# Expert weights as raw float32 in four column tiles of TensorE, 96 token slots per expert

## What is computed

```python
def swiglu(h, w_gate, w_up, w_down):
    return (jax.nn.silu(h @ w_gate) * (h @ w_up)) @ w_down

def moe(h, w_router, w_gate, w_up, w_down):      # h: 256 x 1024
    logits = (h @ w_router).astype(jnp.float32)
    top_l, top_i = lax.top_k(logits, TOP_K)       # 2 of 8
    top_w = jax.nn.softmax(top_l, axis=-1)
    gates = ...                                   # 256 x 8, two entries a row
    y = jnp.zeros_like(h)
    for e in range(N_EXPERTS):                    # w_gate[e], w_up[e]: 1024 x 3584; w_down[e]: 3584 x 1024
        y = y + gates[..., e:e + 1] * swiglu(h, w_gate[e], w_up[e], w_down[e])
    return y
```

## Time and profile before

| | us |
|---|---|
| median of 3 runs (1636.46 to 1638.80) | 1636.68 |
| span of the profiled execution | 1634.3 |
| PE busy | 1602.1 (98%) |
| DVE busy | 1253.7 (77%) |
| ACT busy | 1055.6 (65%) |
| mean rate of the DMA | 278 GB/s |
| first expert matmul starts at | 600.53 |
| last expert matmul starts at | 1621.31 |

### The profile page before, as it was taken

The page is one execution under the profiler, slowest core; times in us unless marked ns, Lnnn a source line. Parts: engine busy times, 40 slices in busy tenths (PEclk is TensorE's granted clock), DMA queues, the critical chain, the costliest instruction groups (busy, mean ns, idle before and its releaser), DMA issues.

```text
span 1634.3 us, 28652 instructions
## 1 busy us (share of the span) xinstructions
PE 1602.1 (98%) x9254; PEld 1368.5 (84%) x9254; DVE 1253.7 (77%) x1418; ACT 1055.6 (65%) x1214; POOL 103.2 (6%) x130
## 2 busy tenths in 40 slices
PE   8999999999999989999999999999999999999997
PEld 7999899998999868887887887888888888888885
DVE  6665755456574669889879889888888988987986
ACT  5454444444554447777777767768777777777874
POOL 0640000000451010000000000000000000000000
PEclk9999999999999979999999999999999999999999
DMA  9654455565554919989998998997997998998980
GB/s 323 214 192 145 144 196 188 187 198 165 186 178 130 335 62 330 378 311 340 377 333 329 374 350 310 373 369 284 382 362 286 384 362 283 382 372 308 350 314 26
DMA packets 230156, 453.95 MB, mean 278 GB/s; under 512 B 8384, under 2 KB 74208, under 8 KB 230112
## 3 DMA queue, kind: packets, MB, share of 16 engines
q1 hardware_dynamic: 230112, 453.33, 77.8%
HBM read 452.26 MB, written 1.05 MB: 277 GB/s over the span
## 4 chain that ended last, share of the span: by engine, by line
PE 96%; DVE 1%; ACT 1%; issue 0%; DMA 0%; POOL 0%; SPq 0%; POOLq 0%; DVEq 0%
PE bank L1195 94%; PE bank L1587 1%; DMA gain<-in_ln_dram 0%; PE bank L1312 0%; POOL rs L1131 0%; DVE mem L696 0%; ACT mem L460 0%; DVE mem L977 0%; ACT w_hi L437 0%; ACT xt_hi L466 0%; DVE x L725 0%; PE bank L1610 0%; PE bank L1228 0%; PE bank L1341 0%; PE bank L1289 0%
## 5 line engine op out<-in xcount | busy, mean ns | idle before, releaser
L663 DVE TENSOR_TENSOR w_lo<-mem,w_hi 128x1024 fp32r<-128x1024 f32 x854 | 1007.0, 1228 | 223.9 <-ACT w_hi L437 222.8
L437 ACT CAST w_hi<-mem 128x1024 fp32r (+1 forms) x854 | 863.9, 1050 | 300.4 <-PE bank L1195 293.1
L1195 PE MATMUL bank<-w_hi,xt_hi 128*128 128x512 f32 (+1 forms) x1088 | 421.5, 387 | 0.9 <-DVE xt_lo L1036 0.9
L1195 PE MATMUL bank<-w_hi,xt_lo 128*128 128x512 f32 (+1 forms) x1088 | 417.2, 383 | 0.0
L1195 PE MATMUL bank<-w_lo,xt_hi 128*128 128x512 f32 (+1 forms) x1088 | 417.1, 383 | 0.0
L1195 PE MATMUL bank<-w_hi,area 128*128 128x512 f32 x1072 | 350.5, 397 | 1.5 <-DVE area L1098 1.5
L1195 PE MATMUL bank<-xt_hi,w_hi 128*128 128x256 f32 x880 | 249.8, 284 | 2.9 <-DVE w_lo L663 2.1
L1195 PE MATMUL bank<-xt_lo,w_hi 128*128 128x256 f32 x880 | 249.3, 283 | 0.0
L1195 PE MATMUL bank<-xt_hi,w_lo 128*128 128x256 f32 x880 | 248.5, 282 | 0.0
L1195 PEld LDWEIGHTS bank<-w_hi,area 128*128 128x128 f32 x1072 | 201.9, 188 | 49.9 <-issue 1.7
L1195 PEld LDWEIGHTS bank<-w_hi,xt_lo 128*128 128x128 f32 x1088 | 205.4, 189 | 44.2
(11 more groups left out here) (173 smaller groups left out, 910.1 us busy)
## 6 DMA issues: line engine op xcount, KB each, us to landing
mem<-in_eg_dram SPq DMA_DIRECT2D x112, 1024.0 KB, 6.5
mem<-in_eu_dram SPq DMA_DIRECT2D x112, 1024.0 KB, 6.5
mem<-in_ed_dram SPq DMA_DIRECT2D x112, 1024.0 KB, 6.4
mem<-in_w_in_dram SPq DMA_DIRECT2D x42, 1024.0 KB, 5.5
mem<-in_fg_dram SPq DMA_DIRECT2D x11, 1024.0 KB, 5.2
mem<-in_fu_dram SPq DMA_DIRECT2D x11, 1024.0 KB, 5.2
mem<-in_fd_dram SPq DMA_DIRECT2D x11, 1024.0 KB, 4.8
mem<-in_w_br_dram SPq DMA_DIRECT2D x8, 1024.0 KB, 4.9
```

The costliest lines, as they stand in the source:

```text
L437: nc.scalar.copy(w_hi[:, q % H, :], src).then_inc(hi_done, 1)
L663: nc.vector.tensor_tensor(w_lo[:, q % H, :], src, w_hi[:, q % H, :].bitcast(F32), ALU.subtract).then_inc(lo_done, 1)
L1195: return nc.tensor.matmul(out, lhs, rhs, start=first, stop=last, skip_group_check=True)
```

## The change

The experts no longer split their weights. PE multiplies raw float32 weights from the ring with raw float32 activations, in float32 matmuls of two passes. SLOTS falls from 128 to 96, in GROUPS = 3 groups of 32 tokens. For a group, the same 32 columns of `ex` are loaded into four column tiles of the array (the output's partitions 32q to 32q+31 name the tile), and each tile streams another quarter (256 columns) of the weights' 1024. A **half** is the new name of a piece of 128 x 1024: it takes 3 groups x 4 tiles = 12 matmuls, 24 passes.

The hidden width is cut in four steps (1024, 1024, 1024 and 512 columns) instead of seven. The ring of the expert stage has RM = 21 halves; neighbouring halves are loaded together in one 1 MB transfer where they lie together, rows are 4 KB (2 KB in the last step, and in all gate and up transfers before), and SP waits for PE's `half_used` where it waited for DVE's `lo_done`. The gather is made of float32 matmuls, without high and low parts; the output is still split in two, and the scatter uses four row tiles of 32 slots. ACT and DVE keep silu, product, copies and the residual. The casts of L589 and L1186 go, and so do the splits of the first pieces; DVE's routing has a few more small operations, since with 96 slots an expert may need three items.

```diff
-SLOTS = 128
+WIDTH = [1024, 1024, 1024, 512]
+HALF = CHUNK // 2
+ITEM_HALVES = 84
+RM = 21
+SLOTS = 96
+GROUPS = SLOTS // 32
...
+            def free_first(n):
+                if n < W_HALVES:
+                    sp.wait_ge(turned, N_TURNED + 6)
+                elif n < RM:
+                    sp.wait_ge(lo_done, 2 * (MOE_BASE // 2 - R + (n - W_HALVES) // 2) + 2)
+                else:
+                    sp.wait_ge(half_used, n - RM + 2)
+            load_item(0, free_first)
+            with sp.Fori(1, NE) as i:
+                load_item(i, lambda n: sp.wait_ge(half_used, ITEM_HALVES * i + n - RM + 2))
...
-            nc.scalar.copy(hn_hi[:, :, :], hn[:, :, :]).then_inc(hn_h, 1)
...
-                    item_split(10, 14, r)
-                    hidden_lo(ESTEPS * i + r + 1)
-                    item_split(14, 20, r)
...
-                                 perm[:, t, :], d == 0 and t == 0, d == 3 and t == TB - 1)
+                        ins = mm(bank[m][:, d * SLOTS:(d + 1) * SLOTS], hn[:, t, dd * P:(dd + 1) * P],
+                                 perm[:, t, :, 0:32].bitcast(F32), d == 0 and t == 0, d == 3 and t == TB - 1)
...
+                for ys in (ys_hi, ys_lo):
+                    for g in range(GROUPS):
+                        at = (g * TB + t) * P
+                        for q in range(4):
+                            rows = slice(32 * q, 32 * q + 32)
+                            ins = mm(bank[4 + q][:, 0:256], perm_t[rows, at:at + P], ys[rows, 256 * g:256 * g + 256],
...
-                            ins = mm3(out[:, :], (ex_hi[:, kk, :], ex_lo[:, kk, :]),
-                                      pair(w, lambda a: a[:, k, :]), kk == 0, kk == KT - 1)
-                        ins.then_inc(piece_used, 1)
...
+                    for c in halves:
+                        w = half(at + c, nk)
+                        for b in range(nk):
+                            kk = nk * c + b
+                            for g in range(GROUPS):
+                                cols = slice(g % 2 * wide, (g % 2 + 1) * wide)
+                                for q in range(4):
+                                    ins = mm(banks[g // 2][32 * q:32 * q + 32, cols], ex[:, kk, 32 * g:32 * g + 32],
+                                             w[:, b, q * wide:(q + 1) * wide], kk == 0 and g % 2 == 0, kk == KT - 1)
+                        ins.then_inc(half_used, 1)
...
+                                ins = mm(bank[4 + g // 2][32 * q:32 * q + 32, cols], eh[s % 2][:, at:at + 32],
+                                         w[:, 0, q * 256:(q + 1) * 256], first and g % 2 == 0, last)
```

More of the change, by code:

```diff
@@ L86, with moe_loads @@
 FFN_PIECES = 6 * STEPS
-ESTEPS = FFE // 512
-ITEM_CHUNKS = 6 * ESTEPS
-ITEM_PIECES = 2 * ITEM_CHUNKS
-SLOTS = 128
+WIDTH = [1024, 1024, 1024, 512]
+OFF = [0, 1024, 2048, 3072]
+ESTEPS = len(WIDTH)
+PART = [w // P for w in WIDTH]
+G_AT = [0, 16, 40, 64]
+U_AT = [8, 24, 48, 68]
+D_AT = [32, 56, 72, 80]
+HALF = CHUNK // 2
+ITEM_HALVES = 84
+RM = 21
+W_HALVES = 9
+MOE_AT = [R * CHUNK + HALF * p for p in range(W_HALVES)] + [CHUNK + HALF * p for p in range(10)] + [0, HALF]
+def moe_loads():
+    edges = set(G_AT + U_AT + D_AT + [ITEM_HALVES])
+    heads, n = {}, 0
+    while n < ITEM_HALVES:
+        p = n % RM
+        size = 2 if n + 1 not in edges and p + 1 < RM and MOE_AT[p + 1] == MOE_AT[p] + HALF else 1
+        heads[n] = size
+        n += size
+    return heads
+MOE_LOADS = moe_loads()
+SLOTS = 96
+GROUPS = SLOTS // 32
+LV = (SEQ - 1) // SLOTS
 EXTRA = (SEQ * TOPK) // (SLOTS + 1)
@@ L228, in trunk @@
         raw_in = [sem(f"raw_in{n}") for n in range(R)]
+        moe_in = [sem(f"moe_in{n}") for n in range(RM)]
+        half_used = sem("half_used")
         hi_done, lo_done, piece_used = sem("hi_done"), sem("lo_done"), sem("piece_used")
@@ L363, in _ @@
                     load_gain(2, ln1_d[1])
[L367 to L396, removed]
@@ L425, in step, with split @@
                 act.wait_ge(act_step, chain[0])
-            def split(q, turn=None, used=None, slot=None):
+            def split(q, turn=None, used=None):
                 c = q // 2
@@ L606, in _ @@
+            gather_copy(1)
             act.wait_ge(routed, 1)
             n_items = act.value_load(items[0:1, 0:1], min_val=NE, max_val=MAX_ITEMS)
-            q0 = MOE_BASE
-            assert cur[0] == q0 + H
-            act.wait_ge(cleared, 1)
             with act.Fori(0, n_items) as i:
[L612 to L628, removed]
-                act.wait_ge(pt_full, i + 1)
-                nc.scalar.copy(perm_t, bank[7][:, 0:SEQ]).then_inc(pt_done, 1)
-                with act.Fori(0, ESTEPS - 1) as r:
-                    item_split(10, 14, r)
[L633 to L640, removed]
-                item_split(ITEM_PIECES - 2, ITEM_PIECES)
@@ L666, in until @@
             def until(q):
-                while cur[0] < q:
+                while cur[0] < min(q, MOE_BASE):
                     n = cur[0]
@@ new lines, in expert_down @@
+                def expert_down(s, halves):
+                    per = WIDTH[s] // 512
+                    for n in halves:
+                        w = half(D_AT[s] + n, 1)
+                        first = s == 0 and n == 0
+                        last = s == ESTEPS - 1 and n == PART[s] - 1
+                        for g in range(GROUPS):
+                            at = (g * per + n % per) * P + 32 * (n // per)
+                            cols = slice(g % 2 * 256, (g % 2 + 1) * 256)
+                            for q in range(4):
+                                ins = mm(bank[4 + g // 2][32 * q:32 * q + 32, cols], eh[s % 2][:, at:at + 32],
+                                         w[:, 0, q * 256:(q + 1) * 256], first and g % 2 == 0, last)
+                        ins.then_inc(half_used, 1)
@@ L1634, in _ @@
-                expert_down(80, ESTEPS * i + ESTEPS, range(2, 4))
-            scatter(0, n_items, 2 * n_items, False)
-            scatter(2, n_items, 2 * n_items)
+                    pe.wait_ge(esg_done, 2 * ESTEPS * i + 2 * ESTEPS)
+                    for m in range(2):
+                        gather(m)
+                expert_down(ESTEPS - 2, range(2, 4))
+                transposes(ESTEPS - 1)
+                expert_down(ESTEPS - 2, range(4, PART[ESTEPS - 2]))
+                pe.wait_ge(eh_done, ESTEPS * i + ESTEPS)
@@ L1639 @@
+                expert_down(ESTEPS - 1, range(PART[ESTEPS - 1]))
+            scatter(0, n_items + 1)
+            pe.wait_ge(scat_done, 4 * n_items + 2)
+            scatter(1, n_items + 1)
 def kernel(**inputs):
```

379 lines of the change are left out of this document (186 added, 193 removed).

## The result

The changed kernel takes 1646.67 us (median of 4 runs, 1644.63 to 1648.36), against 1636.57 us for the kernel before beside it: a ratio of 1.0056, 95% interval 1.0044 to 1.0068. It is slightly slower, by 0.6%. The forecast was 1575 us and faster. The profiled execution spans 1643.9 us with a mean granted clock of 0.979.

The account below looks back on a forecast made before the run. PE's own work was taken to bound the expert stage. Stage start 597.5, eight items 962.4 and tail 12.8 gave 1572.7, plus 2.4 from span to median: 1575 us, range 1530 to 1700.

Parts of the forecast that it names:

- Part 1: Expert matmuls: 504 passes of four tiles at 0.218 us, 109.9 us an item against 117.9 before.
- p: Expert matmuls: time of one 256-column pass of four side-by-side tiles, taken as 0.218 us, ends 0.212 and 0.249.
- the steady row: Profile row of two alternating 64x64 tiles with 128 columns: 0.106 us a pass, 0.212 us for 256 columns.
- the untiled one: Profile row of four untiled float32 passes of 256 columns: a step of 0.249 us.
- Parts 2 and 3: Rest of an item, 10.4 us against 9.7; expert stage starting about 3 us earlier, at 597.5 us, and tail of 12.8 us.
- Part 4: Expert weight transfers: 341.3 MB at mean 378 GB/s take 903 us, hidden behind PE's 962 us with a 6% margin.
- the rival on the transfers: Expert stage: DMA pressed to 350 GB/s bounds it, time 1591 us; at 362, 1562; still faster, chance 0.08.
- the rival on the clock: Tiled expert work: PE's clock stays low as from 576 to 606 us, p doubles, about 2450 us; chance 0.03.
- 504 x 0.218: Expert matmuls of one item: 84 x 6 = 504 four-tile passes at 0.218 us, 109.9 us.
- Loads or issue show: Expert matmuls: weight loads or instruction issue slow the tiled passes; at a 0.249 us step, 1700 us; slower, chance 0.06.
- 64 passes at 0.014 us: Profile row cited against the loads or issue rival: 64 tiled passes took 0.014 us each, loads included.
- "Slower": Whole kernel: summed chance of a slower result, 0.10 + 0.06 + 0.03 + 0.01 = 0.20.

Follow-up runs that it names:

- the version that fetches unhindered: The changed kernel with PE's loop over items written out and three quarters of each expert weight transfer's columns left out from the second expert on; 1565.63 us, one run.

## Why the prediction was wrong

**Right, Part 1.** p = 0.2168 us against 0.218. The four tiles run side by side with 256 columns; the choice of the steady row over the untiled one was the right one.

**Right, Parts 2 and 3, with small errors.** The gather takes 3.74 us (3.6), a scatter's half 0.91 us and six transposes 0.80 us with their joints. PE's floor of an item is 119.5 us (120.3): eight items, 6.4 us less than forecast. The first expert matmul starts at 595.82 us (597.5): the gather ahead of it took 5.44 us and not 6.93 again. The tail is 13.9 us (12.8), with a wait for DVE ahead of each half of the scatter:

```profile
1619.45 10.57 PE L1204 MATMUL bank<-mem 128*32 128x256 f32 x192
1631.78 0.98 PE L1204 MATMUL bank<-area 32*128 32x256 f32 x24 [1.76 <-DVE area L1079]
1634.62 1.46 PE L1204 MATMUL bank<-area 32*128 32x256 f32 x24 [1.86 <-DVE x L1088]
```

**Wrong in size, Part 4.** The transfers did not bound it; the rate when full is 408, not 378 GB/s, so the margin was 14% and not 6% (341.3 MB in eight items of 119.5 us ask for 357 GB/s). In the rival on the transfers, 362 GB/s gives 1558.5 us by that same sum and not 1562; either is below 1575. In the rival on the clock, was read too simply: between 582 and 588 us the granted clock was 1.00 once more. Nothing hangs on either.

**The step that failed: the sum has no term for PE's program.** "504 x 0.218" counted passes and compared them with as many matmuls, as if they were as many instructions. A step of four tiles is four passes and four loads where there was one of each: an item went from some 1160 matmuls and loads (456 matmuls in 100 us, each with its load) to 4630, in a loop that was held and is so no longer. Its price in the changed kernel is 55.0 us for seven jumps (1646.67 - 1591.65) and 26.0 us for the dense last step (1591.65 - 1565.63). The forecast's own terms were 9.4 us too high (1575 - 1565.63, a single run). So 1575 - 9.4 + 26.0 + 55.0 = 1646.6; the sum closes by construction, as each term is a difference between neighbouring runs. What speaks for the terms is the trace of the changed kernel: of the 81.0 us, 62.1 are waits that the profile can't name, and slow clock stands behind each jump.

The rival "Loads or issue show" came near, with the wrong measure. It was argued down with 64 passes at 0.014 us: a burst of 128 instructions, half a packet, in which nothing stalled. That row tells how fast PE can issue what it has, and nothing of how fast more arrives: here a half with 96 instructions would need a packet every 3.5 us (256 x 1.32 / 96) for ten microseconds on end. Two rows of the profile of before would have raised the question: q8 with 31 packets for the whole execution, when PE's 9254 matmuls and as many loads are 72 packets of instructions, so most of them were carried out from what PE held; and the DMA at 0.95, on which new packets have to find room. The range held the time (1530 to 1700) by luck: its upper end stood for another cause, matmuls that are slow one by one. "Slower" had a chance of 0.20, and none of it for this.

**The sign.** The gain on PE is there: 70.9 us (1636.57 - 1565.63, the version that fetches unhindered). The price is 81.0 us. The 10 us between them, the result, say little of either.

## What to carry to other kernels

Count the instructions of a loop's body, not only its passes, whenever a change makes tiles smaller: a body over 1260 to 1690 PE instructions was fetched anew in each turn here. Each jump then cost some 3.8 us in the kernel before and 7.8 to 7.9 us in the changed one, slow clock included; writing the loop out removes it, and dense stretches are to be spread between wide passes. Read the row of the instruction queue, and take "issue" as a cause, or a named wait that stands exactly at a jump, as a reason to compare packets.

## What the runs showed of the hardware that was not expected

- PE's loop was held at about 1260 instructions and fetched anew at about 1690, 2510 and 5020, with two to three packets of 16 KB beyond the body at each jump.
- The gap at a jump was 2.4 to 2.7 us with matmuls of 512 columns, 5.4 to 6.8 us with four tiles and full weight traffic, and 3.5 to 4.1 us with a quarter of it; in the last two cases a jump cost the same, 7.8 to 7.9 us. That fewer instructions per microsecond make the shorter gap is likely, but no run varied that alone.
- Straight on, PE kept up at 48 instructions in 1.30 us beside full weight traffic, and at 96 in 1.32 us only with a quarter of the traffic.
- Four column tiles of float32 run side by side: 0.2168 us for four passes of 256 columns at 2.4 GHz, against 0.212 for two alternating tiles.
- Rows of 4 KB (2 KB in one step of four) moved 408 GB/s on one core.
